# Thirteen dense chunks of a two-block transformer kernel as seven block products instead of eight, with the rotation's sine product moved to POOL

## The reference, cut to what matters

```python
h = rmsnorm(x, norm_pre_g)                    # [2048, 1024]
z = jnp.einsum('bsd,de->bse', h, w_in)        # w_in: [1024, 4096]
A, C = ATTN_WIDTH, CONV_WIDTH_2               # 768, 256
cuts = np.cumsum([A, A, A, A, C, C, C])
q, k, v, g_attn, c_h, c_b, c_c, g_conv = jnp.split(z, cuts, axis=-1)
q = rope(q.reshape(B, S, N_ATTN_HEADS, HEAD_DIM), pos)     # t1*cos - t2*sin, t2*cos + t1*sin
k = rope(k.reshape(B, S, N_ATTN_HEADS, HEAD_DIM), pos)
...                                           # dilated window attention, gated by silu(g_attn)
conv_out = c_b * causal_depthwise_conv(c_c * c_h, conv_w)
conv_out = conv_out * jax.nn.silu(g_conv)
y = jnp.einsum('bse,ed->bsd', jnp.concatenate([attn_out, conv_out], axis=-1), w_out)
x = x + rmsnorm(y, norm_post_g)
```

## Time and profile before

| | us |
|---|---|
| median of 3 runs (2238.70, 2242.82, 2241.88) | 2241.88 |
| span of the profiled execution, first to last instruction | 2236.8 |
| the profiled execution's own time | not given apart from its span |
| PE busy | 2059.5 (92%) |
| DVE busy | 1394.6 (62%) |
| ACT busy | 925.3 (41%) |
| POOL busy | 912.2 (41%) |
| PE of the rope and gate stages: first matmul at, first matmul of attention at | 1074.11, 1622.42 |

### The profile page before, as it was taken

The page is one execution under the profiler, slowest core; times in us unless marked ns, Lnnn a source line. Parts: engine busy times, 40 slices in busy tenths (PEclk is TensorE's granted clock), DMA queues, the critical chain, the costliest instruction groups (busy, mean ns, idle before and its releaser), DMA issues.

```text
span 2236.8 us, 43330 instructions
## 1 busy us (share of the span) xinstructions
PE 2059.5 (92%) x16228; PEld 1509.7 (67%) x16228; DVE 1394.6 (62%) x3479; ACT 925.3 (41%) x2009; POOL 912.2 (41%) x1004
## 2 busy tenths in 40 slices
...
GB/s 183 141 113 63 104 82 39 90 146 197 152 113 105 89 134 126 123 124 72 128 139 121 111 116 62 121 56 63 53 126 167 207 202 194 172 205 148 161 177 85
DMA packets 285536, 279.95 MB, mean 125 GB/s; under 512 B 39712, under 2 KB 237216, under 8 KB 285072
## 3 DMA queue, kind: packets, MB, share of 16 engines
...
...
HBM read 171.22 MB, written 93.31 MB: 118 GB/s over the span
## 4 chain that ended last, share of the span: by engine, by line
PE 31%; DVE 21%; POOL 11%; issue 5%; DMA 3%; ACT 3%; SPq 2%; DVEq 0%; ACTq 0%; POOLq 0%
PE bank L173 20%; PE bank L2641 7%; DVE s2m L2491 6%; DVE p2l L2497 4%; POOL xr L1776 2%; POOL xr L1763 2%; POOL xr L1761 2%; POOL xr L1778 2%; SPq L1964 1%; DMA qr<-qf 1%; PE bank L1405 1%; DVE qf L1933 1%; DVE qr L1931 1%; DVE qf L1930 1%; ACT s2sh L1915 1%
## 5 line engine op out<-in xcount | busy, mean ns | idle before, releaser
L173 PE MATMUL bank<-xh,w2h 128*128 128x512 f16 x640 | 243.3, 380 | 0.0
L173 PE MATMUL bank<-xl,w2h 128*128 128x512 f16 x640 | 243.2, 380 | 0.0
L173 PE MATMUL bank<-xh,w2l 128*128 128x512 f16 x640 | 243.1, 380 | 0.0
L173 PE MATMUL bank<-w2h,xh 128*128 128x256 f16 x768 | 210.4, 274 | 14.6 <-DVE xl L638 13.6
L173 PE MATMUL bank<-w1h,xh 128*128 128x256 f16 x768 | 211.0, 275 | 3.0 <-DVE s1st L937 3.0
L173 PE MATMUL bank<-w1h,xl 128*128 128x256 f16 x768 | 210.8, 275 | 0.0
L173 PE MATMUL bank<-w1l,xh 128*128 128x256 f16 x768 | 210.8, 274 | 0.0
L173 PE MATMUL bank<-w2l,xh 128*128 128x256 f16 x768 | 210.4, 274 | 0.0
L173 PE MATMUL bank<-w2h,xl 128*128 128x256 f16 x768 | 210.3, 274 | 0.0
L2436 PE MATMUL bank<-ident,p2r 128*128 128x128 f32 x900 | 163.7, 294 | 49.0 <-DVE p2l L2497 41.8
L260 POOL TENSOR_TENSOR size<-size,power 128x1 f32<-128x1 f32 x15 | 8.6, 570 | 398.3 <-DVE size L254 398.3
...
## 6 DMA issues: line engine op xcount, KB each, us to landing
...
v<-scr_v SPq DMA_DIRECT2D x192, 65.0 KB, 2.7
...
qr<-qf SPq DMA_DIRECT2D x192, 64.0 KB, 2.0
...
```

The source lines that it names most:

```text
L173: ins = nc.tensor.matmul(dst, x, y, start=k == 0 and m == 0, stop=k == n - 1 and m == 2)
```

## The change

**The scheme.** The rows are taken in two pairs P of 1024 (each two blocks of 512), the inner size in two halves of 512 and a chunk's columns in two halves of 128. Each chunk and pair is then a product of 2 x 2 blocks, eight block products before, now seven (Strassen's scheme in Winograd's form) with sums of blocks in front and behind. A block product is 12 matmuls of 512 columns in form "f", and 48 of 128 columns in form "n". Chunks 0 to 2 keep the old form.

**Sums of activations** (T1 to T4 of each pair) are made once, at the end of the norm stage: `dve_pair` on DVE (nine operations of 2048 elements a pair), a cast on ACT and a subtraction on POOL for each of the four; T1 takes the place of one block of `xh` and `xl`. Chunk 2's groups are reordered for that.

**Sums of weights** (S1 to S4) are made for each of the 13 chunks: `act_prep` and `pool_prep` in eight steps replace `pool_split`. POOL now has four additions of 512 elements and six subtractions (one of 1024, five of 512), ACT six casts.

**Sums of products.** Three PSUM banks a pair: products 3 to 6 go on top of what stands in a bank once it has been read. DVE (and ACT for two) combines banks with the intermediate tiles m1, u2 and u4. The stages are written out by `slots_of`: one **slot** is one block product, 14 to a chunk, and each engine's work is placed by the slot.

**The rest.** In the rope stage the sine product is on POOL, and tiles come in the order of `CORNERS`. The old gate stage is split: `mix_stage` (chunks 9 to 12) and `gate_stage` (13 to 15), with one more hand-over between them. Where buffers lie is left out below.

```diff
+        def pool_prep(self, n, step):
...
+            def rest(name):
+                src, hi, lo = p[name]
+                nc.gpsimd.tensor_tensor(lo, src, hi, ALU.subtract).then_inc(*self.g_w.up())
+            def add(i, x, y, op):
+                nc.gpsimd.tensor_tensor(self.sums[:, i], x, y, op).then_inc(*self.g_w.up())
...
+                add(0, a11, a21, ALU.subtract)
+                add(1, a21, a22, ALU.add)
...
+    SEVEN = ((0, 0, "B11"), (4, 1, "T2"), (5, 2, "T3"), (3, 1, "T1"), (1, 0, "B21"), (6, 1, "B22"), (2, 2, "T4"))
+    CORNERS = (("C22", 1, 1), ("C11", 0, 0), ("C12", 0, 1), ("C21", 1, 0))
+    def pe_product(kind, wts, n, i, xs, bank):
+        (wh, wl), (op, _, name) = wts.parts(n), SEVEN[i]
+        xh, xl = xs[name]
+        for u in range(1 if kind == "f" else 4):
+            dst, cols = (bank[:], slice(0, 512)) if kind == "f" else (bank[:, 128 * u:128 * u + 128], slice(128 * u, 128 * u + 128))
+            for k in range(4):
+                for m, (w, x) in enumerate(((wh, xh), (wh, xl), (wl, xh))):
+                    a, b = w[:, op, k, :], x[:, k, cols]
+                    ins = nc.tensor.matmul(dst, *((a, b) if kind == "f" else (b, a)), start=i < 3 and u == k == m == 0,
+                                           stop=k == 3 and m == 2, skip_group_check=True)
+        return ins
...
+        if late:
+            work += [("split", 2), ("pair", 0, "T4"), ("group", 1, 3), ("pair", 0, "T3"), ("load", 3), ("pair", 1, "T1"), ("group", 2, 1),
+                     ("kept", 0), ("total", 3), ("pair", 1, "T2"), ("scaled", 3), ("bound", 3), ("group", 2, 3), ("prep", 3, 0), ("pair", 1, "T4"),
+                     ("prep", 3, 1), ("prep", 3, 2), ("group", 2, 0), ("fit", 3), ("prep", 3, 3), ("prep", 3, 4), ("pair", 1, "T3"),
+                     ("kept", 1), ("prep", 3, 5), ("prep", 3, 6), ("prep", 3, 7), ("group", 2, 2)]
...
+        def dve_pair(P, name):
...
+            steps = {"T1": ((B12[0], B11[0], ALU.subtract), (s1, B12[1], ALU.add), (s1, B11[1], ALU.subtract)),
+                     "T2": ((B22[0], s1, ALU.subtract), (s2, B22[1], ALU.add)),
+                     "T4": ((B21[0], s2, ALU.subtract), (t["T4"], B21[1], ALU.add)),
+                     "T3": ((s2, B11[0], ALU.subtract), (t["T3"], B11[1], ALU.subtract))}[name]
...
+            for x, y, op in steps:
+                dve.wait_ge(*d_tx.now())
+                nc.vector.tensor_tensor(t[name], x, y, op).then_inc(*d_tx.up())
...
+    def slots_of(n_chunks, outs, after, weights):
+        work, due = [], {}
+        for at in range(14 * n_chunks + 8):
+            i, s = divmod(at, 7)
+            if i < 2 * n_chunks:
+                work.append(("mul", i, s))
+                if s in (1, 2):
+                    work.append((("t", i), ("u2", i))[s - 1])
+                if s == 4:
+                    work.append(("u4", i))
+            done = (i - 1, 3) if s == 0 else (i, s - 4) if s >= 4 else None
+            if done is not None and 0 <= done[0] < 2 * n_chunks:
+                work += [(x, *done) for x in outs]
+                for later, what in after:
+                    due.setdefault(at + later, []).append((what, *done))
+            work += due.pop(at, [])
+            if i < 2 * n_chunks:
+                work += [(what, at // 14, *more) for slot, what, *more in weights if slot == at % 14]
+        for at in sorted(due):
+            work += due[at]
+        return work
+    PREPARE = [(0, "load"), (0, "sum"), (1, "total"), (3, "scaled"), *((4 + k, "prep", k) for k in range(8))]
...
-        qf, qr = sbs("qf", 3, [128, 512], F32, scope), sbs("qr", 2, [128, 512], F32, scope)
+        qf, qr = sbs("qf", 5, [128, 512], F32, scope), sbs("qr", 3, [128, 512], F32, scope)
+        m1, u2, u4 = (sb(n, [128, 512], scope=scope) for n in ("m1", "u2", "u4"))
+        work = slots_of(6, ("out",), ((1, "sin"), (2, "turn"), (3, "half"), (4, "rest")),
+                        PREPARE + [(5, "bound"), (7, "pbound"), (9, "fit")])
...
+                    if s == 0:
+                        pe.wait_ge(*wts.ready[first + n])
+                    pe.wait_ge(*xs_ready[P].get(SEVEN[s][2], before))
+                    pe.wait_ge(*(before if s < 3 else (d_u.at(5 * i + 1), a_t.at(i + 1), d_u.at(5 * i + 2), d_u.at(5 * i + 3))[s - 3]))
+                    pe_product("f", wts, first + n, s, xs[P], bank).then_inc(*p_mm.up())
...
+        def dve_add(dst, i, bank, mm, to):
+            dve.wait_ge(*p_mm.at(7 * i + mm))
+            dve.wait_ge(*d_u.now())
+            nc.vector.scalar_tensor_tensor(dst[:], trio[i][bank][0][:], fits.fit[:, i // 2:i // 2 + 1], to[:], ALU.mult, ALU.add).then_inc(*d_u.up())
...
+                    q, c = qf[m % 5], tiles[m]["c"]
+                    dve.wait_ge(*made(m))
+                    dve.wait_ge(*r_in[m % 3].at(64 * (m // 3 + 1)))
+                    dve.wait_ge(*c_in.at(32))
+                    nc.vector.tensor_tensor(q[:], q[:], cosT[:, c:c + 512], ALU.mult).then_inc(*d_rp.up())
+                    dve.wait_ge(*d_rp.now())
+                    dve.wait_ge(*g_sn.at(m + 1))
+                    nc.vector.tensor_tensor(q[:], q[:], qr[m % 3][:], ALU.add).then_inc(*d_rp.up())
+                elif item[0] == "rest":
...
+                if item[0] == "sin":
+                    m = 4 * item[1] + item[2]
+                    c = tiles[m]["c"]
+                    pool.wait_ge(*r_in[m % 3].at(64 * (m // 3 + 1)))
+                    pool.wait_ge(*c_in.at(32))
+                    nc.gpsimd.tensor_tensor(qr[m % 3][:], qr[m % 3][:], sinT[:, c:c + 512], ALU.mult).then_inc(*g_sn.up())
...
+    def mix_stage(scope, wts, first, xs):
...
+                    pe_product("n", wts, first + n, s, xs[P], bank).then_inc(*p_mm.up())
...
+    chunks2 += [chunk("f", [(at + 256 * c, 256)], False, scale, True) for at, scale in ((Q2, -0.125), (K2, 1.0)) for c in range(3)]
+    for c in range(2):
+        chunks2 += [chunk("f", [(H2 + 128 * c, 128), (C2 + 128 * c, 128)], seven=True), chunk("f", [(B2 + 128 * c, 128), (GC2 + 128 * c, 128)], seven=True)]
+    chunks2 += [chunk("n", [(G2 + 256 * c, 256)], seven=True) for c in range(3)]
...
+            rope_stage(s2, wts, 3, xs, xs_ready, fits)
+            wait_all(hand_over())
+        with stack() as s2:
+            mix_stage(s2, wts, 9, xs)
             wait_all(hand_over())
```

More of the change, by code:

```diff
@@ L356, in norm_stage @@
             work.append(("turn", g))
+            if late and g == 3:
+                work.append(("pair", 0, "T1"))
             if g == 0:
```

857 lines of the change are left out of this document (583 added, 274 removed).

## The result

| | before | after |
|---|---|---|
| median of the runs, us | 2242.11 | 2289.99 (2289.01 to 2293.28) |
| ratio, 95% interval | | 1.022 (1.0201 to 1.0239) |
| span of the profiled execution, us | 2236.8 | 2288.1 |
| first matmul of chunk 3 at | 1074.11 | 1113.87 |
| chunks 3 to 8, us | 256.0 | 275.3 |

The change makes the kernel 48 us slower. The forecast was 2270 (range 2215 to 2296): the direction and the places of the losses are right, the sum is 20 us short. The profile before is, by its span, that of the fastest run (2238.70), the one after that of a middle one (2289.88), so between the two profiles the difference is 51.3 us. All of it but 0.9 lies in the stretch that the change touches: +39.8 ahead of chunk 3, +19.3 in the rope stage, -8.7 behind it, +50.4 in all.

A forecast was written before the change was run, and what follows sets the result against it. PE's matmuls were taken to set the pace before the change. Terms 39.5 + 12 - 7.9 + 18 - 20.8 - 13.2 gave +27.6 us on the 2236.8 span, 2264.4; with the median 5.1 above, 2270, range 2215 to 2296.

The forecast's parts named there:

- start of chunk 3: Norm stage's end: PE waits for the weights' and activations' sums, first product at 1111 instead of 1074.11, +37 us.
- slower start behind it: Start of chunk 3: what PE loses when it starts again after the wait, 2.5 us.
- rope stage, with the 7.9 lost before: Rope stage: six chunks 261 us instead of 249, +12; 7.9 us lost there before are inside the new figure, -7.9.
- hand-overs and attention's start: Both hand-overs: PE's weights' total waits for ACT's sum, 10.9 and 4.4 us; with restarts and attention's start +18.
- mix and gate products: Mix and gate stages: four "f" chunks at 36.3 us, -20.8; three "n" chunks at 37.5 us, -13.2.
- the exclusion: Norm and rope stages: DVE operations with two SBUF inputs and POOL operations exclude each other, the later waits.
- The bound by sums alone: Norm stage's end: DVE's and POOL's operations one at a time, 90.2 us, chunk 3 at 1100 at the earliest, +26.
- the rival of 46 us a chunk: Rope stage: combinations late in both pairs, 46 us a chunk, +15 more, 2285; chance 0.17.
- the addition for k: Rope stage: k chunks 44.2 us against 42.7 for q, as eight rests are 0.33 longer and half shows.
- 128 columns don't pay: Last three chunks: unhidden weight loads make 87 ns a matmul, 58.5 us a chunk, 2333; chance 0.05.
- As drawn: Whole change: one engine's stalls fall where the other has slack, -62 us, 2180; chance 0.12.
- the port alone: Norm and rope stages: exclusive port but always filled, norm +26, rope 236, 2221; chance 0.14.

The follow-up runs named there:

- e2: Changed kernel with the eight rests of the activations' sums at the norm stage's end on DVE instead of POOL: 2276.23 us, ratio 1.0158.
- e3: Changed kernel with POOL's sums and rests for the weights of chunks 5 to 9 made for 32 columns only: 2259.89 us, ratio 1.0082.
- e9: Changed kernel with sine and chunks 4 to 9's weight sums and rests on DVE, three store buffers, bound's reduction at slot 12: 2258.37 us, ratio 1.0074.

## Why the forecast came out as it did

| term | forecast | measured |
|---|---|---|
| start of chunk 3 | +37 | +39.8 |
| slower start behind it | +2.5 | +2.8 (in the rope stage's length: 1.65 by the clock, 1.2 by ACT's sum) |
| rope stage, with the 7.9 lost before | +4.1 | +16.5 |
| hand-overs and attention's start | +18 | +26 |
| mix and gate products | -34.0 | -33.9 |

The measured terms add up to the 51.3 us between the two profiles, within rounding. The forecast added up to 27.6; 3.2 of the 23.7 us between them don't reach the median, because I put it 5.1 us above the profile's span and it lies 1.9 above. So the range, 2215 to 2296, held with 6 us to spare, and the time came out at the upper edge of the forecast's own 2250 to 2290.

*What bounds, and the exclusion.* Right. A pair of operations of 2048 elements takes the sum of its durations in the trace after (1050.55 to 1057.00, 6.45 us for 4.07 and 2.28), a pair of 512 columns 1.67 us, somewhat under it; e2 shows that work moved from POOL to DVE shortens the stage, e3 and e9 that POOL's operations are what lengthens DVE's.

*The norm stage's end.* Right in place, mechanism and size: 40 us for 37, and the tail of 13.6 us for 13.5. The bound by sums alone (26) was too low: there are stretches like the one before 1085.88 in which neither DVE nor POOL has such an operation while a sum is with ACT.

*The rope stage.* The mechanism was right, the term was mis-sized by 12 us. The places of the waits were right for the second pair (fourth product 2.5 to 4.8 us for the 3.2 taken). In chunks 4 to 8 the second pair waits 4.5 and 0.7 us in the mean, 5.2 together for the 5.9 taken. Two things were missing. Waits in the first pair, 1.0 to 2.4 us ahead of the fourth product and up to 1.7 ahead of the sixth, where I had said none: 13 us in all. And what stands behind a wait: I had put 0.5 us a chunk for PE's slower start. The rows at 1236.63 show steps of 0.37 and then 0.43 us, and the product behind the long wait lasts 1.4 to 2.5 us more than 2.6, 9.6 us in five chunks. Of the 1.5 us more for a k chunk 0.9 showed (45.8 for chunks 4 and 5, 46.6 for 6 to 8, in the mean); in e9 it is 2.3. By its length, the rival of 46 us a chunk, which had 0.17, is what came, and its condition, late combinations in the first pair too, was met; the second pair still lost twice as much as the first (26 and 13 us). It was priced at 2285, and 8 us more at the hand-overs less the 3.2 of the median make 2290. Inside this term something cancels: the waits of the second pair (5.9 for 5.2) and the addition for k were too large and hid some 6 us of what was missing.

*The hand-overs.* The first was 14.6 and 2.5 (wait and slow product) for 10.9 and 1.2, the second 6.2 and 2.1 for 4.4 and 1.2; attention's start cost 0.8 for 0.7. The chain was right, link by link (store to sum 3.6 us of ACT idle, sum 1.9), but it started late: DVE was still turning tiles of the pair before when the last product ended, so the last rest ended at 1403.9, 14.7 us behind PE, and the sum 19.2 us behind PE where I had 13.5. Of this PE covered two products, 5.2 us, and not the one of 2.6 that I had taken: the total stands behind the second.

*The products.* Right. The rival "128 columns don't pay" is out: 56 ns for 672 matmuls in a row. The Trainium skill's 81 ns ("TensorE: Matmul & The Clock Gate", "Back-to-back issue gap") was not met: the two chunks behind the hand-over took 37.7 and 37.5 us, where it would make an estimated 54.4, and the first took 45.8 with its wait.

*"As drawn" and "the port alone"* are out: chunk 3 at 1113.9 and no chunk under 43.9.

The terms that were off were all too small. My reading, which no run isolates, is that each was computed with queues that start on time, and each queue was late by what the one before had lost; at the first hand-over the rows show it.
